# Two hybrid layers on one core: Exp per head with its own sum, value matmuls over four heads at once, and an expert stage that adds x at its end

## The chip, the cores and the metric

The program runs as one launch on one core of a Trainium2 chip. The metric is the device time of that launch in microseconds (us), as the median of several executions. A core has a matrix engine (TensorE, PE in the profile, with its weight loads as PEld), a vector engine (DVE), a scalar engine (ACT), GpSimd (POOL) and a queue engine that here only starts DMAs (SP). Each runs its own list of instructions in order; semaphores tie them together. Working memory is SBUF (128 partitions); matmuls write to PSUM, eight banks of 128 x 512 float32.

## The reference, cut to what matters

Activations are 256 tokens of width 1024 (`N`, `D`), kept with the features on the partitions as eight tiles of 128 x 256 (`KD` = 8). A first network of two layers (feed-forward, Fourier mixer, retention) runs first, then a second network of two layers. Only the second is changed. One of its layers does, in order:

```
u = rmsnorm(x, ln1);   p = u @ w_in                       # ProjectIn
attention, 2 groups of 4 heads, 4 branches                 # Attention
    s = q k^T / 8 + bias                                   # compressed, selected, window: gated
    w = exp(s - max(s)) / sum(exp(s - max(s)))             # sliding window with a sink per head:
    o = sum over the branches of gate * w @ v              #   max and sum include the sink
rwkv branch;  merge of the branches;  x = x + merged @ w_out
z = rmsnorm(x, ln2)                                        # expert_norm
route: top 16 of 128 x 128 keys per head                   # PeerRoute, PeerGates
x = x + sum over 128 blocks of (gates * gelu(z @ U_b)) @ V_b   # PeerExperts
```

After the second layer comes a last rmsnorm, and its result is the output.

## The kernel before, in words

The program is a list of stages (`second_network`, L2676). Each stage has one method per engine, and each engine runs the methods of all stages one after the other. `stage_done` counts finished stages; most methods begin by waiting for it. All large products are split into float32r parts: `product` (L240) issues three matmuls (L243 to L245) where one would do: rounded weights by rounded input, rounded weights by the input's rest, rest of the weights by rounded input. Weights come as blocks of 1 MB through a ring of four, loaded by SP; ACT rounds a block (L231, in `lead` ahead of a stage's start) and POOL subtracts to get the rest (L259).

`Attention` (L1302) works in 16 units: for each tile of 128 queries (t = 0, 1) and each group g of four heads there are the branches CMP (15 compressed keys), SEL, WIN and SWA. A unit's width is 15 keys for CMP, otherwise 128 keys at t = 0 and 256 at t = 1. PE issues, for u = 0 to 15, `scores(u + 3)` (L1411), `turn(u)`, which transposes the weights (L1423), and `values(u - 1)` (L1443), which does something only after WIN (with CMP, SEL and WIN summed in PSUM) and after SWA. DVE issues `shift(u + 1)` ahead of `weigh(u)`: shift is scale and bias (L1544), maximum (L1546), for CMP a clamp (L1548), for SWA the sink (L1551, L1552), and the subtraction (L1553); weigh is the sum (L1562) and four-number operations (L1564 to L1572). ACT issues `exp(u + 2)` (L1471), `keep(u)` (L1478), which copies the transposed weights out of PSUM, and `keep_sum(u - 1)` (L1487). POOL multiplies the weights by their scale (L1588). Scores are plain float32, so each matmul of attention appears in the trace as two records.

`Norm` (L448) squares x on ACT (L488), sums on PE (L519, L522), takes the root on ACT (L493) and the reciprocal on DVE (L543), scales (L559), rounds on ACT (L507) and takes the rest on DVE (L552). Where the stage before is a `Project`, its ACT part is early: it starts with each pair of tiles of x. Otherwise it waits for the whole stage.

The experts sum into PSUM banks 4 to 7, two tiles of x per bank. Before, `expert_norm` puts x there first with four matmuls by the identity (L531), because it then overwrites the other half of `chip.x`; all 128 blocks add to it without closing the sum; at the end four matmuls by a block of zeros close the banks (L2586), and one DVE copy moves all eight tiles to `chip.x` (L2663). The stage `LoadTables` (L1183) then starts two DMAs from ACT, for masks and the bias table of attention, ahead of the next norm.

## Time and profile before

| | |
|---|---|
| median of 3 runs | 5032.56 us (5031.7 to 5032.76) |
| the profiled execution | 5030.94 us |
| its span, first to last instruction | 5028.8 us |
| PE busy | 4589.3 us, 91% of the span |
| DVE / ACT / POOL busy | 33% / 34% / 56% |
| attention of the second network, layer 0 | about 2174 to 2286 us |
| attention, layer 1 | about 3704 to 3817 us |
| last expert matmul of layer 0 / layer 1 | ends at about 3480.0 / 5007.9 us |

The profile is of one execution, and its times are from the span's start. In the rows, a line number is a line of this kernel; "idle" and the arrow say how long an engine stood still before an instruction and what released it. PEclk is the granted clock of TensorE as a share: 0.50 is 1.2 GHz and 1.00 is 2.4 GHz.

### The profile page before, as it was taken

The page shows a single profiled execution, that of the slowest core. Times are in us where ns is not written, and L with a number is a line of the kernel's source. Part 1 is how long each engine was busy: PE and PEld are TensorE (multiplying, and loading weights), DVE is VectorE, ACT ScalarE, POOL GpSimd, SP SyncE. Part 2 cuts the span into 40 slices and gives each one's busy share as a digit, 9 for nine tenths or more (in the row PEclk, how much of TensorE's full clock was granted, in tenths as well). Part 3 has the DMA queues.
Part 4 walks back from the last instruction along what each step waited for, and adds up shares of the span by engine and source line. Part 5 has one row for each costly group of instructions (what it writes and reads, how often), then busy time and mean ns, then how long its engine had stood idle before and what let it go on. Part 6 is the DMA issues. An engine that isn't in the chain of part 4 may idle for free.

```text
span 5028.8 us, 73099 instructions
## 1 busy us (share of the span) xinstructions
PE 4589.3 (91%) x30266; PEld 4143.0 (82%) x30266; DVE 1634.7 (33%) x3051; ACT 1727.8 (34%) x2481; POOL 2802.4 (56%) x1354
## 2 busy tenths in 40 slices
PE   7998999999999898998857999999998866999998
PEld 5777677787788798977857999998977865999998
DVE  2211221121114321464577111112454668111112
ACT  3223222222232343421224444444431233444443
POOL 3342343344344386720467888886730367888886
PEclk9999999999999899967888999999976888999999
DMA  6623364222232244410120555554420130454543
GB/s 259 233 92 84 117 247 163 84 101 92 84 109 101 84 168 163 168 67 1 59 101 22 180 182 184 184 182 174 167 100 1 48 112 1 176 184 183 180 181 141
DMA packets 94372, 648.52 MB, mean 129 GB/s; under 512 B 9824, under 2 KB 16224, under 8 KB 16608
## 3 DMA queue, kind: packets, MB, share of 16 engines
q1 hardware_dynamic: 87120, 633.21, 34.6%
q10 hardware_dynamic: 7056, 12.49, 1.1%
q8 instruction: 148, 2.42, 0.2%
q14 instruction: 48, 0.39, 0.0%
HBM read 641.46 MB, written 4.19 MB: 128 GB/s over the span
## 4 chain that ended last, share of the span: by engine, by line
PE 83%; DVE 12%; ACT 2%; issue 1%; POOL 1%; DMA 1%; SPq 0%; ACTq 0%; DVEq 0%; POOLq 0%
PE ps L243 23%; PE ps L244 23%; PE ps L245 22%; PE ps L2505 3%; PE ps L1443 2%; PE ps L398 1%; PE ps L1411 1%; DVE arena L2075 1%; DVE x L729 1%; PE ps L1762 1%; PE ps L1809 1%; PE ps L971 1%; DMA arena<-in_mod_weights 1%; PE ps L1423 1%; PE ps L1815 1%
## 5 line engine op out<-in xcount | busy, mean ns | idle before, releaser
L259 POOL TENSOR_TENSOR ring_rest<-ring,rounded 128x1024 fp32r<-128x1024 f32 x1032 | 2508.2, 2453 | 1635.6 <-ACT rounded L231 1366.7
L243 PE MATMUL ps<-part,rounded 128*128 128x256 f32 (+1 forms) x5760 | 1839.6, 319 | 108.0 <-DVE part L552 46.6
L244 PE MATMUL ps<-part,rounded 128*128 128x256 f32 (+1 forms) x5760 | 1827.5, 317 | 0.0
L245 PE MATMUL ps<-part,ring_rest 128*128 128x256 f32 (+1 forms) x5760 | 1826.0, 317 | 0.0
L243 PEld LDWEIGHTS ps<-part,rounded 128*128 128x128 f32 x5760 | 1111.3, 193 | 213.3 <-DVE part L552 43.5
L245 PEld LDWEIGHTS ps<-part,ring_rest 128*128 128x128 f32 x5760 | 1110.8, 193 | 68.8
L244 PEld LDWEIGHTS ps<-part,rounded 128*128 128x128 f32 x5760 | 1111.9, 193 | 66.9
L231 ACT ACTIVATE rounded<-ring 128x1024 fp32r<-128x1024 f32 x528 | 527.5, 1050 | 700.4 <-PE ps L245 693.5
L243 PE MATMUL ps<-x_parts,rounded 128*128 128x256 f32 x2304 | 655.9, 285 | 9.6 <-DVE x_parts L552 8.1
L2623 ACT ACTIVATE rounded<-ring 128x1024 fp32r<-128x1024 f32 x504 | 531.5, 1054 | 373.6 <-DMA ring<-in_weights 366.5
L244 PE MATMUL ps<-x_parts,rounded 128*128 128x256 f32 x2304 | 654.2, 284 | 0.0
L245 PE MATMUL ps<-x_parts,ring_rest 128*128 128x256 f32 x2304 | 654.1, 284 | 0.0
L243 PEld LDWEIGHTS ps<-x_parts,rounded 128*128 128x128 f32 x2304 | 444.4, 193 | 12.2 <-DVE x_parts L552 10.4
L244 PEld LDWEIGHTS ps<-x_parts,rounded 128*128 128x128 f32 x2304 | 444.6, 193 | 0.0
L245 PEld LDWEIGHTS ps<-x_parts,ring_rest 128*128 128x128 f32 x2304 | 444.6, 193 | 0.0
L2653 DVE TENSOR_TENSOR ps<-ps,arena 128x256 f32<-128x256 f32 x256 | 160.1, 625 | 680.0 <-ACT ps L2602 680.0
L2656 DVE TENSOR_TENSOR part<-ps,part 128x256 fp32r<-128x256 f32 x256 | 108.8, 425 | 520.4 <-ACT part L2608 520.4
L648 ACT ACTIVATE arena<-ps 128x512 f32<-128x512 f32 (+1 forms) x88 | 47.9, 544 | 617.8 <-PE ps L245 617.8
L662 DVE TENSOR_TENSOR part<-ps,arena 128x512 f32<-128x512 f32 (+1 forms) x88 | 55.0, 625 | 562.9 <-ACT arena L648 562.9
L2602 ACT ACTIVATE ps<-ps 128x256 f32<-128x256 f32 x256 | 94.2, 368 | 413.2 <-PE ps L245 413.2
L729 DVE SCALAR_TENSOR_TENSOR x<-ps,mods_of_layer,x 128x256 f32<-128x256 f32 x80 | 31.9, 476 | 512.0 <-PE ps L245 512.0
L2161 POOL TENSOR_TENSOR part<-arena,part 128x1024 fp32r<-128x1024 f32 x6 | 14.4, 2402 | 294.1 <-ACT part L2141 294.1
(325 smaller groups left out, 4408.3 us busy)
## 6 DMA issues: line engine op xcount, KB each, us to landing
ring<-in_weights SPq DMA_DIRECT2D x528, 1024.0 KB, 4.8
arena<-in_mod_weights SPq DMA_DIRECT2D x72, 1024.0 KB, 7.8
arena<-bias_scratch ACTq DMA_DIRECT2D x2, 2048.0 KB, 8.7
bias_scratch<-arena ACTq DMA_DIRECT2D x1, 3072.0 KB, 32.8
x<-in_x SPq DMA_DIRECT2D x1, 2048.0 KB, 10.0
arena<-in_keys ACTq DMA_DIRECT2D x2, 1024.0 KB, 5.0
arena<-in_cst SPq DMA_DIRECT2D x1, 1216.0 KB, 28.2
arena<-in_expo ACTq DMA_DIRECT2D x1, 1024.0 KB, 4.8
```

The source lines that it names most:

```text
L231: self.nc.scalar.activation(c.rounded[:, s % ROUNDED, half], c.ring[:, slot, half], ACT.Copy)\
L243: mm(out, w[0], a[0], start=start, stop=False)
L244: mm(out, w[0], a[1], start=False, stop=False)
L245: return mm(out, w[1], a[0], start=False, stop=stop)
L259: eng.tensor_tensor(c.ring_rest[:, slot, half], c.ring[:, slot, half], c.rounded[:, (self.s0 + r) % ROUNDED, half].bitcast(F32), ALU.subtr ...
L729: last = self.nc.vector.scalar_tensor_tensor(c.x[:, m, cols], c.ps[:, m, cols], gate, c.x[:, m, cols], ALU.mult, ALU.add)
L1443: last = nc.tensor.matmul(ps[:, 6 + n % 2, i * P:(i + 1) * P], v, weights, start=k == 0, stop=k == len(parts) - 1)
L2505: last = self.nc.tensor.matmul(self.chip.ps[:, n % self.BANKS, i * P:(i + 1) * P], self.hot[:, n % self.BUFS, 0, i], self.hot[:, n % self. ...
L2602: copy(self.hidden(r), c.ps[:, r % 2, 0:N], ACT.Gelu).then_inc(self.gelu_ready.sem, 1)
L2623: self.nc.scalar.activation(c.rounded[:, (self.s0 + r) % ROUNDED, half], c.ring[:, f % RING, half], ACT.Copy)\
L2653: v.tensor_tensor(gelu, gelu, self.gates[:, :, bass.ds(b, 1)].rearrange("p t a -> p (t a)"), ALU.mult)\
L2656: v.tensor_tensor(self.parts[1][:, r % 2, :], gelu, self.parts[0].bitcast(F32)[:, r % 2, :], ALU.subtract)\
```

## The change

Attention: the subtraction of the maximum is gone from DVE; the maximum is taken with its sign turned and given to ACT as the bias of Exp, and since a bias is one number per partition, Exp is issued once for each of the four heads, each with an accumulator output that is the sum over the keys. DVE's sum is gone as well. The value matmuls take all four heads' weights as one moving operand of 512 columns instead of four of 128.

Experts: x is no longer put into PSUM. `expert_norm` copies it in SBUF (seven tiles into the arena, the eighth over the modulation table, which is now one tensor for both layers and no longer needed by then). Four float32r matmuls with zeros open the banks before the first block adds to them. The last block closes its sums itself and signals after each bank, and DVE adds x tile by tile. A norm behind the experts is early, as behind a `Project`. `LoadTables` is no stage any more; its two DMAs are issued by ACT at the end of the norm.

```diff
@@ Norm
-        early = isinstance(self.before, Project)
+        early = isinstance(self.before, (Project, PeerExperts))
...
-        if self.keep:
-            act.wait_ge(self.x_kept.sem, self.x_kept.at(1))
...
+        if self.tables:
+            self.tables.issue(act)
...
-        if self.keep:
-            for b in range(4):
-                last = mm(c.ps[:, 4 + b, :].rearrange("p (m n) -> p m n", m=2), c.ident, c.x[:, 2 * b:2 * b + 2, 0:N],
-                          start=True, stop=False)
-            last.then_inc(self.x_kept.sem, 1)
...
         dve.wait_ge(self.chip.stage_done, self.index)
+        for tiles, kept in self.kept or ():
+            nc.vector.tensor_copy(kept, c.x[:, tiles, 0:self.t])
         dve.wait_ge(self.summed.sem, self.summed.at(1))
@@ Attention
-            for i in range(4):
...
-                for k, (v, weights) in enumerate(parts):
-                    last = nc.tensor.matmul(ps[:, 6 + n % 2, i * P:(i + 1) * P], v, weights, start=k == 0, stop=k == len(parts) - 1)
+            for k, (v, weights) in enumerate(parts):
+                last = nc.tensor.matmul(ps[:, 6 + n % 2, :], v, weights.rearrange("p i t -> p (i t)"),
+                                        start=k == 0, stop=k == len(parts) - 1)
...
-            e = self.sc[:, u % self.BUFS, :, 0:self.width(t, b)]
-            nc.scalar.activation(e, e, ACT.Exp).then_inc(self.exped.sem, 1)
+            for i in range(4):
+                e = self.sc[:, u % self.BUFS, i, 0:self.width(t, b)]
+                last = nc.scalar.activation(e, e, ACT.Exp, bias=st[:, 0, i:i + 1], accum_out=st[:, 1, i:i + 1])
+            last.then_inc(self.exped.sem, 1)
...
-            link(v.tensor_reduce(st[:, 0, :], sc, AX.X, ALU.max))
+            last = v.tensor_reduce(st[:, 0, :], sc, AX.X, ALU.max, negate=True)
...
-            v.tensor_tensor(sc, sc, st[:, 0, :].unsqueeze(2).broadcast_to([P, 4, w]), ALU.subtract)\
-                .then_inc(self.shifted.sem, 1)
+            last.then_inc(self.shifted.sem, 1)
...
             dve.wait_ge(self.exped.sem, self.exped.at(u + 1))
-            link(v.tensor_reduce(st[:, 1, :], sc, AX.X, ALU.add))
@@ PeerExperts
+def kept_input(chip):
+
+    most = KD - 1
+    mods = chip.all_mods[:].rearrange("p l a d s -> p (l a d s)")[:, 0:N].rearrange("p (d n) -> p d n", d=1)
+    return [(slice(0, most), chip.at(G_KEPT, most, N)), (slice(most, KD), mods)]
...
+                if end and m % 2 and m < KD - 1:
+                    last.then_inc(self.closed.sem, 1)
...
+            if r == 1:
+                pe.wait_ge(self.zeroed.sem, self.zeroed.at(1))
+                for bank in range(4, 8):
+                    nc.tensor.matmul(c.ps[:, bank, :], self.zero[:, 0:P], self.zero, start=True, stop=False)
...
-        for bank in range(4, 8):
-            last = nc.tensor.matmul(c.ps[:, bank, :], self.zero, c.cst[:], start=False, stop=True)
-        last.then_inc(self.closed.sem, 1)
...
-        dve.wait_ge(self.closed.sem, self.closed.at(1))
-        v.tensor_copy(c.x[:, :, 0:N], c.ps[:, 4:8, :].rearrange("p b (m n) -> p (b m) n", n=N)).then_inc(c.stage_done, 1)
+        for m in range(KD):
+            if m == KD - 2:
+                dve.wait_ge(c.block_done, self.block_count(self.blocks - 1))
+            elif m % 2 == 0:
+                dve.wait_ge(self.closed.sem, self.closed.at(m // 2 + 1))
+            for tiles, x in self.kept:
+                if tiles.start <= m < tiles.stop:
+                    v.tensor_tensor(c.x[:, m, 0:N], x[:, m - tiles.start, :], self.out(m), ALU.add)\
+                        .then_inc(self.x_ready.sem, 1)
```

The places in the order of instructions on which the steps of the prediction rest follow, before and then now. Names of tiles: `ps` is PSUM, `arena` the SBUF work area, `part` a float32r tile in it, `cst` the constants. Line numbers of the changed kernel differ slightly.

PE in attention at t = 1 from the scores of unit 13 (L1411) to the values behind the last unit (L1443):

```order
L1411 MATMUL ps<-arena 128x256 x4
L1423 MATMUL ps<-cst,arena 128x128 x8
L1443 MATMUL ps<-arena 128x128 x20
L1411 MATMUL ps<-arena 128x256 x4
L1423 MATMUL ps<-cst,arena 15x128 x4
L1443 MATMUL ps<-arena 128x128 x8
L1423 MATMUL ps<-cst,arena 128x128 x24
L1443 MATMUL ps<-arena 128x128 x28
```

```order
L1407 MATMUL ps<-arena 128x256 x4
L1419 MATMUL ps<-cst,arena 128x128 x8
L1438 MATMUL ps<-arena 128x512 x5
L1407 MATMUL ps<-arena 128x256 x4
L1419 MATMUL ps<-cst,arena 15x128 x4
L1438 MATMUL ps<-arena 128x512 x2
L1419 MATMUL ps<-cst,arena 128x128 x24
L1438 MATMUL ps<-arena 128x512 x7
```

The order is the same; each group of value matmuls has a quarter of its number, with four times the columns.

DVE at the same stretch: shift of the sliding-window unit 11, weigh of unit 10, then shift of unit 12.

```order
L1544 SCALAR_TENSOR_TENSOR arena<-ps,arena 128x1024
L1546 TENSOR_REDUCE arena<-arena 128x4
L1551 TENSOR_TENSOR arena<-arena,vec 128x4
L1552 TENSOR_TENSOR arena<-vec,arena 128x4
L1553 TENSOR_TENSOR arena<-arena 128x1024
L1562 TENSOR_REDUCE arena<-arena 128x4
L1566 TENSOR_SCALAR arena<-arena 128x4
L1567 RECIPROCAL arena<-arena 128x4
L1572 TENSOR_TENSOR arena<-arena 128x4
L1544 SCALAR_TENSOR_TENSOR arena<-ps,arena 128x4x15
```

```order
L1543 SCALAR_TENSOR_TENSOR arena<-ps,arena 128x1024
L1545 TENSOR_REDUCE arena<-arena 128x4
L1552 SCALAR_TENSOR_TENSOR arena<-vec,arena 128x4
L1553 TENSOR_TENSOR arena<-vec,arena 128x4
L1564 TENSOR_SCALAR arena<-arena 128x4
L1565 RECIPROCAL arena<-arena 128x4
L1570 TENSOR_TENSOR arena<-arena 128x4
L1543 SCALAR_TENSOR_TENSOR arena<-ps,arena 128x4x15
```

Two of the four wide operations between one unit's scores and the other unit's scale are gone (L1553 and L1562 of before). On ACT the one Exp of each unit became four, in the same place.

DVE at the end of the experts and in the norm behind them:

```order
L2663 COPY x<-ps 128x8x256
L541 COPY arena<-ps 128x256
L543 RECIPROCAL ps<-arena 128x256
L559 SCALAR_TENSOR_TENSOR arena<-x,vec,ps 128x256 x8
L2789 UNCONDITIONAL_BRANCH
```

```order
L2679 TENSOR_TENSOR x<-arena,ps 128x256 x7
L2679 TENSOR_TENSOR x<-mods,ps 128x256
L540 COPY arena<-ps 128x256
L542 RECIPROCAL ps<-arena 128x256
L558 SCALAR_TENSOR_TENSOR arena<-x,vec,ps 128x256 x8
```

The one wide copy became eight adds of one tile each, of which six wait only for the first three banks.

## Rows read from the trace of the kernel before

**Rows 1.** Two stretches of attention: length, busy per engine, PEclk, DMA share, GB/s

```profile
2174.00:2286.00 112.00, 102.94 (x392) 82.98 (x392) 60.40 (x124) 27.24 (x44) 18.73 (x16) 0.55 0.01 3
3740.00:3760.00 20.00, 20.00 (x56) 13.99 (x56) 9.79 (x16) 3.90 (x5) 3.22 (x3) 0.50 0.00 0
```

**Rows 2.** Order of time, PE, attention: start, length, instruction, idle before

```profile
2186.77 1.11 PE L1423 MATMUL ps<-cst,arena 128*128 128x128 f32 x4 [1.16 <-POOL arena L1588]
2219.04 7.56 PE L1443 MATMUL ps<-arena 15*128 15x128 f32 x24
2238.25 1.09 PE L1423 MATMUL ps<-cst,arena 128*128 128x128 f32 x8 [1.33 <-POOL arena L1588]
2244.52 10.98 PE L1443 MATMUL ps<-arena 15*128 15x128 f32 x40
2259.96 3.62 PE L1443 MATMUL ps<-arena 128*128 128x128 f32 x16
2267.14 1.97 PE L1423 MATMUL ps<-cst,arena 128*128 128x128 f32 x8 [2.63 <-POOL arena L1588]
```

**Rows 3.** Chain that ended last behind layer 0's experts: start, length, where

```profile
3480.00 3.45 PE ps L2586 x8
...
3483.48 2.30 DVE x L2663
...
3486.75 0.13 ACT arena L488
...
3488.94 1.89 ACT rounded L231 x2
...
3492.14 0.48 ACT arena L493
```

**Rows 4.** The same behind the experts of layer 1, to the end

```profile
5007.90 3.45 PE ps L2586 x8
...
5018.87 0.48 ACT arena L493
```

**Rows 5.** The chain through the norm ahead of the routing, layer 0

```profile
2530.06 3.45 PE ps L531 x8
...
2533.98 2.39 DVE x_parts L552
```

**Rows 6.** Order of time, DVE, around unit 11

```profile
2230.35 1.22 DVE L1544 SCALAR_TENSOR_TENSOR arena<-ps,arena 128x1024 f32<-128x1024 f32 x1 [6.76 <-PE ps L1411]
2233.25 1.23 DVE L1553 TENSOR_TENSOR arena<-arena 128x1024 f32<-128x1024 f32 x1
2234.40 1.21 DVE L1562 TENSOR_REDUCE arena<-arena 128x4 f32<-128x1024 f32 x1
```

**Rows 7.** Order of time, ACT: four pieces with bias; then around exp 15

```profile
2147.80 1.57 ACT L1843 ACTIVATE arena<-ps,vec 128x256 f32<-128x256 f32 x4 [2.20 <-PE ps L1670]
2263.62 0.59 ACT L1487 ACTIVATE arena<-ps 64x512 f32<-64x512 f32 x1 [2.83 <-PE ps L1443]
2264.21 1.04 ACT L1471 ACTIVATE arena<-arena 128x1024 f32<-128x1024 f32 x1
2265.15 1.00 ACT L1478 ACTIVATE arena<-ps 128x1024 f32<-128x1024 f32 x1
```

**Rows 8.** PEclk around the values of unit 11, in stretches of 2 us

```profile
2260.00:2262.00 2.00, 2.00 (x11) 2.00 (x11) 1.90 (x4) 0.59 (x1) 0.00 (x0) 0.50 0.00 0
2264.00:2266.00 2.00, 0.52 (x5) 0.28 (x3) 1.73 (x5) 2.00 (x4) 0.80 (x1) 1.00 0.00 0
```

**Rows 9.** Order of time where a norm is early already, behind a Project

```profile
1945.19 0.28 PE L245 MATMUL ps<-part,ring_rest 128*128 128x256 f32 x1
1946.32 0.63 ACT L488 ACTIVATE arena<-x 128x512 f32<-128x512 f32 x1 [0.15 <-DVE x L729]
1948.96 0.47 ACT L493 ACTIVATE arena<-ps,vec 128x256 f32<-128x256 f32 x1 [0.71 <-PE ps L522]
```

**Rows 10.** Order of time, first expert block to sum into PSUM

```profile
2748.26 0.36 PE L243 MATMUL ps<-part,rounded 128*128 128x256 f32 x1 [0.71 <-DVE part L2656]
```

More of the change, by code:

```diff
@@ L131, in __init__ @@
         self.headones, self.iota = self.cst[:, 2, :], self.cst[:, 3, :]
-        self.mods = [self.place(f"mods_of_layer{i}", [P, N_MOD, KD, 2])[0] for i in range(DEPTH)]
+        self.all_mods, = self.place("mods", [P, DEPTH, N_MOD, KD, 2])
+        self.mods = [self.all_mods[:, i] for i in range(DEPTH)]
         self.ps = ctx.enter_context(nc.psum_tensor("ps", [P, 8, 512], F32))
@@ L454, with __init__ @@
     TILE = 32
-    def __init__(self, chip, out, sq, small, tokens, bank, mod=None, gain=None, parts=None, keep=False, mods=None, lead=None):
+    def __init__(self, chip, out, sq, small, tokens, bank, mod=None, gain=None, parts=None, kept=None, tables=None, mods=None,
+                 lead=None):
         super().__init__(chip)
-        self.t, self.mod, self.gain, self.keep = tokens, mod, gain, keep
+        self.kept, self.tables = kept, tables
+        self.t, self.mod, self.gain = tokens, mod, gain
         self.mods, self.first_mods = mods, lead
@@ L2563, in up, with down @@
             last.then_inc(self.up_done.sem, 1)
-        def down(it, r):
+        def down(it, r, end=False):
             b = it * RING + r
@@ L2645, in dve @@
         dve.wait_ge(self.chip.stage_done, self.index)
-        v.memset(self.zero, 0.0).then_inc(self.zeroed.sem, 1)
+        v.tensor_scalar(self.zero, c.cst[:].rearrange("p a n -> p (a n)"), 0.0, None, ALU.mult).then_inc(self.zeroed.sem, 1)
         def body(it, first=False):
@@ L2681, in second_network @@
         tables = LoadTables(chip, start)
-        stages += [tables, second_norm(chip, columns(vec, "ln1", layer, KD), split=True), ProjectIn(chip),
+        stages += [second_norm(chip, columns(vec, "ln1", layer, KD), split=True, tables=tables), ProjectIn(chip),
                    Attention(chip, layer, tables), Rwkv(chip, layer)]
```

56 lines of the change are left out of this document (29 added, 27 removed).

## The prediction, made before the changed kernel ran

> **What bounds the kernel now.** I read the page first: PE is busy for 91% of the span and holds 83% of the chain that ended last, so a change pays only where it shortens PE's own work or a stretch in which PE stands. Then I looked at attention in windows, because all that the change does to DVE and ACT lies there. It takes 112 us per layer, and PE is busy for 102.9 of them, at a mean granted clock of 0.55; a piece of 20 us has PE busy throughout at 0.50, which is 1.2 GHz [rows 1]. So attention is bound by a slowly clocked PE, with a few waits. PE's timeline names these: it waits for POOL, 1.16 us near the start, 1.33 us ahead of turn 10 and 2.63 us ahead of turn 14 [rows 2]. Last come the chains behind the experts, where PE has nothing to do: from the last expert product to the root of the next norm there are 12.1 us in layer 0 and 11.0 us in layer 1 [rows 3, 4].
>
> **Values, four heads at once.** Two rows give the price of a record. 24 records take 7.56 us and 40 take 10.98 [rows 2]; both contain eight records with a stationary tile of 15 rows, so 16 full ones cost 3.42, or 0.214 each, and the eight cost 0.517 each, 0.30 more, which I read as a weight load that isn't hidden when the number of rows changes. Afterwards the groups have 6 and 10 records of 512 columns, two of them with 15 rows. The trace has such a record at 2.4 GHz: eight in 3.45 us, 0.431 each [rows 5], hence 0.863 at 1.2 GHz. 6 x 0.863 + 2 x 0.30 = 5.8 and 10 x 0.863 + 0.6 = 9.2: 1.77 us less each. There are four such groups per layer (units 2, 6, 10, 14): 7.1 us per layer. The sliding-window groups only swap 16 x 0.214 for 4 x 0.863, nothing. Bounds at an unchanged clock: 0.6 less per group if the penalty is paid per column and not per load, 0.6 more if it vanishes; 4.7 to 9.5 per layer.
>
> **DVE, ACT and the waits.** Unit 11 shows why PE waits. Its shift can start only with its scores at 2230.35, and weigh of unit 10 stands behind it in DVE's queue, so L1553 (1.23) and L1562 (1.21) both lie between the scores and the scale of unit 10 [rows 6]. Both go, about 2.4 us. Against that ACT issues four Exps. Four 256-column activations with a bias take 1.57 together [rows 7], against 1.04 for the one Exp now. What an accumulator output adds isn't in this trace. It can't be under 0 (0.39 per piece), and the nearest row for one more small activation, L1843's own 0.39, gives 0.8 per piece as the other end. I take 0.15 more, 0.55 per piece, 2.2 per unit at 256 keys, because it moves four bytes per partition. Behind exp on ACT's queue stand keep and keep_sum; turn of the next unit waits for keep. So:
> - Start: DVE no longer paces the first units; the wait of 1.16 goes. ACT needs less than 3 us per unit there, PE as much. Gain 1.2.
> - Turn 10: weigh 10 is ready 2.4 earlier; ACT starts exp 11 when unit 7's keep_sum is out, ends it 2.2 later and then keeps unit 9, just before PE comes. Gain 1.3.
> - Turn 14: here ACT takes over. exp 15 starts behind keep_sum 11 (2263.62), now 2264.21, and keep 13 (2265.15) stands behind it [rows 7]. With 2.2 in place of 1.04 keep 13 ends at about 2267.3, and turn 14 began at 2267.14. So of 2.63 us of wait nothing comes back: 0.
> Per layer 2.5, with ends of -1.5 (0.8 per piece) and 4.
>
> **The clock inside attention.** PE busy isn't enough for 2.4 GHz: 20 us at full busy share were granted 0.50 [rows 1]. It does rise during the 16 records of unit 11's values, dense and with 128 rows: 0.50 at 2260, 1.00 at 2264 [rows 2, 8]. In the 40 records ahead of them, interrupted eight times, it doesn't. Merged, the full rows stand together: 8 x 0.863 = 6.9 us in one piece for unit 10, and 10.4 for units 14 and 15, against 3.6 at unit 11. I expect the clock to rise inside both. For unit 10 that saves 1 to 2 us in the values, up to 1.9 in the scores of unit 15 and some of the chain behind; for the last group 2 to 3. The shorter groups of units 2 and 6 (3.4 us dense) may go either way. I take 5.5 per layer from ends of 0 and 12. The Trainium skill ("TensorE: Matmul & The Clock Gate", section "What's actually happening") says that a hardware monitor sets the clock by how busy PE has been and that activity releases the throttle. Read as busy time this is not what the trace shows [rows 1], and by it merging would change nothing in the clock: that is the first rival below.
>
> **Behind the experts.** In layer 0 the last product ends at 3480.00; then come the closing matmuls (3.45), the copy (2.30), 0.97 in which ACT issues the tables' DMAs, the squares, two roundings, a table load and the root at 3492.14 [rows 3]: 12.14 us. Afterwards three banks are closed before the last product ends, and two adds remain, as behind a Project. There the last product ends at 1945.31, the last square runs from 1946.32 to 1946.95 and the root starts at 1948.96 [rows 9]. So the squares end 1.64 after the products, and what follows the squares on ACT is unchanged, 3492.14 - 3488.94 = 3.20 [rows 3]: the root comes at 4.84, 7.3 earlier. At the end there is no rounding: 5018.87 - 5007.90 = 10.97 becomes 3.65, again 7.3 [rows 4, 9]. The norm that opens the second network loses only the DMA issues, 0.9. The DMAs themselves now start at the end of ACT's norm and still have some 200 us until attention; behind them in ACT's queue stand only roundings whose slots aren't free yet. 15.5 together.
>
> **Ahead of the routing, and the zeros.** L531 (3.45) held ACT's first rounding until 2533.5, so that the first rest started at 2533.98 and then stood for 2.39 beside POOL's subtraction [rows 5]. Without it the rest can slip in ahead of that operation of POOL, and PE gets one tile of the queries earlier, though at 1.2 GHz and with the next tile as late as before: 0.7 per layer. The two copies on DVE fill a gap there of about 1.4 us with some 1.3; if they don't fit, the gain is gone (0) or a whole POOL operation, 2.4, is lost once per layer. The four zero matmuls stand ahead of the first sum into PSUM, where PE waits 0.71 us for DVE now [rows 10]; each is one pass over 512 columns where the records of 0.43 [rows 5] are two, so 0.22 to 0.43 each, 0.9 to 1.7 less 0.7 together: I take 0.2 per layer. Together 1.0.
>
> **Sum.** 2 x (7.1 + 2.5 + 5.5) = 30.2 in attention, 15.5 behind the experts, 1.0 for the rest: 46.7. From the profiled execution's 5030.94 that is 4984.2; the median of the runs shown lies 1.6 above that execution, so I predict 4986.
>
> **Rivals.**
> - *The clock stays.* The scores with their 64 rows and the turns break the dense pieces, or the monitor looks at something that merging leaves as it is. For: no rise in 20 us of full busy share. Against: the rise at unit 11. 11 us less gain: 4997.
> - *ACT takes the place of DVE.* Each Exp piece with its accumulator costs about 0.95, more than twice a plain piece. Then exp 15 takes 3.8, keep 13 ends 1.8 us later than turn 14 began, turn 10 is 0.3 later, and the first units run at ACT's pace, 2 later: the waits cost 4 per layer where I gain 2.5. 13 us less: 4999, or 5004 if the clock suffers too.
> - *The clock rises in all four groups* and stays for the scores between them. For: merged, the full rows of units 2 and 6 are 3.5 us in one piece, about what unit 11 has now. Against: their scores of 64 rows come right behind. 8 us per layer more: 4970.
> - *Slower than before.* One mechanism only has the size: ACT bounds attention as a whole. It issues 64 Exp pieces per layer, beside what it does now, 27.2 us at most [rows 1]. To eat the other terms (15.5 and 1.0) and 10 us more, attention would have to last 13 us longer per layer, 125 us, so (125 - 27) / 64 = 1.5 us per piece, four times the 0.39 of a plain one. A table load ahead of each piece would do it, but the order of instructions has one load per layer there. It would give 5043, and decides from 1.5 us per piece.
>
> **How the numbers follow.** Forecast 0.62, clock stays 0.17, ACT 0.09, clock everywhere 0.08, slower 0.02, something unseen 0.02. The range of 8 in 10 takes in the first two whole and most of the next: 4968 to 5003. A measurement of this kernel tells 0.2% (10 us) from no change; nearly all cases are beyond it: faster 0.96, same 0.02, slower 0.02.
>
> **What would show it.** Right: value records of 0.86 us at 0.50, six and ten to a group; PEclk near 1.00 in the later half of unit 10's values; no wait ahead of turn 10, a wait for ACT's keep ahead of turn 14; Exp pieces of 0.4 to 0.8; the root 4.8 and 3.7 us behind the last expert product; attention at 95 to 99 us. Wrong: attention above 105, pieces near 1 us, or a first query product that isn't earlier against the norm's root.

## The result, and the profile after

The changed kernel takes 4960.16 us (median of 4, 4957.67 to 4961.43), against 5032.66 for the kernel before on the same chip: ratio 0.9855, interval 0.9838 to 0.9872. That is 72.5 us less where I forecast 46.7, and below my range. The profiled execution took 4957.67, its span 4955.9, 72.9 less than before. By milestones of the two traces, forecast in the last column:

| stretch | before | after | difference | forecast |
|---|---|---|---|---|
| start to last square behind the first network's last Project | 1946.32 | 1944.32 | -2.0 | 0 |
| to the first scores of layer 0 | 229.3 | 227.4 | -1.9 | -0.9 |
| attention, layer 0 | 110.5 | 84.3 | -26.2 | -15.1 |
| to the last product ahead of the routing's norm | 240.7 | 241.8 | +1.1 | 0 |
| to the first query product | 9.6 | 10.1 | +0.5 | -0.7 |
| to the last expert product | 943.6 | 942.9 | -0.7 | +0.2 |
| to the first product of layer 1 | 17.3 | 9.9 | -7.3 | -7.3 |
| to the first scores of layer 1 | 208.0 | 208.1 | +0.1 | 0 |
| attention, layer 1 | 112.0 | 81.3 | -30.8 | -15.1 |
| to the last expert product | 1190.6 | 1192.2 | +1.6 | -0.5 |
| to the end | 20.9 | 13.6 | -7.3 | -7.3 |

Attention is the whole miss: 57.0 against 30.2. Its windows, first the layer 0 stretch and then layer 1 (columns as in [rows 1]), and layer 1 of before, which [rows 1] lacks:

```profile
2171.00:2256.00 85.00, 78.35 (x260) 48.96 (x260) 34.77 (x91) 43.33 (x156) 18.75 (x16) 0.69 0.00 1
3669.00:3750.00 81.00, 75.18 (x260) 46.89 (x260) 34.56 (x88) 42.98 (x156) 18.75 (x16) 0.71 0.00 1
```

```profile
3705.00:3817.00 112.00, 103.86 (x392) 83.81 (x392) 59.50 (x121) 27.23 (x44) 18.74 (x16) 0.55 0.00 1
```

DVE's work fell from 60 to 35 us, ACT's rose from 27 to 43, and the granted clock rose from 0.55 to 0.69 and 0.71. Length times clock gives attention in microseconds at full clock: 112.0 x 0.55 = 61.6 before, 85.0 x 0.69 = 58.7 and 81.0 x 0.71 = 57.5 after. At the old mean clock of 0.55 these would be 106.7 and 104.5 us. So by this reckoning 5 and 7 us per layer are less work and waiting, and the rest of 26 and 31, some 21 and 23, is clock. (It is rough: a wait does not scale with the clock.) Over the whole span the clock records of the two traces give 758 us at 1.2 GHz before and 653 after; half of the difference, 52.6 of the 72.9 us, is clock. PE in layer 0, in order of time, columns as in [rows 2], which these answer:

```profile
2171.73 7.19 PE L1407 MATMUL ps<-arena 64*128 64x15 f32 x32 [6.14 <-DVE arena L1526]
2181.63 1.11 PE L1419 MATMUL ps<-cst,arena 128*128 128x128 f32 x4
...
2188.77 5.78 PE L1438 MATMUL ps<-arena 15*128 15x512 f32 x6
...
2211.52 5.78 PE L1438 MATMUL ps<-arena 15*128 15x512 f32 x6
2217.23 1.99 PE L1407 MATMUL ps<-arena 64*128 64x256 f32 x8
...
2225.53 1.06 PE L1419 MATMUL ps<-cst,arena 128*128 128x128 f32 x8 [0.97 <-ACT arena L1477]
...
2229.47 4.75 PE L1438 MATMUL ps<-arena 15*128 15x512 f32 x10
...
2242.30 1.06 PE L1419 MATMUL ps<-cst,arena 128*128 128x128 f32 x8 [3.03 <-ACT arena L1477]
2244.57 1.94 PE L1419 MATMUL ps<-cst,arena 128*128 128x128 f32 x8 [1.21 <-ACT arena L1477]
...
2256.01 0.66 PE L1738 MATMUL ps<-cst,arena 128*128 128x128 f32 x4 [0.73 <-ACTq L1500]
```

The reader is to see that the values of units 2 and 6 take the forecast 5.8 at 1.2 GHz, that scores of 256 keys behind unit 6 take 1.99 and no longer 3.78, so the clock is up 45 us behind the first scores and stays up through the values of units 10 and 11 and the scores of unit 15; and that the wait ahead of turn 14 is there, now for ACT. Behind that wait the clock falls: the last turn takes 1.94 for 1.06.

Behind the experts of layer 0 (chain that ended last), and at the end of the program; they answer to [rows 3, 4]:

```profile
3448.84 2.92 DVE x L2679 x8
...
3452.32 1.99 ACT rounded L232 x2
...
3455.61 0.48 ACT arena L495
```

```profile
4942.22 0.28 PE L246 MATMUL ps<-part,ring_rest 128*128 128x256 f32 x1
4942.43 2.20 PE L521 MATMUL ps<-arena,cst 128*32 128x256 f32 x16
4942.87 0.41 DVE L2679 TENSOR_TENSOR x<-mods,ps 128x256 f32<-128x256 f32 x1
...
4945.96 0.47 ACT L495 ACTIVATE arena<-ps,vec 128x256 f32<-128x256 f32 x1 [0.71 <-PE ps L524]
```

The last products of the two layers are done at 3450.81 and 4942.35 (a record's successor begins 0.12 to 0.13 behind it): the root comes 4.8 and 3.6 later, forecast 4.8 and 3.7.

Ahead of the routing my gain of 0.7 became a loss of 0.5. The chain that ended last there, and POOL beside it:

```profile
2495.52 2.88 DVE x L728 x8
...
2498.55 2.02 DVE arena L538
2500.57 2.00 DVE mods L538
2502.57 0.34 DVE arena L540
...
2503.70 0.48 ACT arena L495
...
2508.22 2.13 DVE x_parts L551
```

```profile
2500.08 4.70 POOL L260 TENSOR_TENSOR ring_rest<-ring,rounded 128x1024 fp32r<-128x1024 f32 x2 [7.67 <-ACT rounded L232]
```

The copy of seven tiles begins before POOL does and takes 2.02 us; the eighth, a seventh of that, takes 2.00, until the first of POOL's two operations (4.70 / 2, begun at 2500.08) is over.

### The profile page after: what moved, and what is told of

The parts are those of the page before. It is cut to its first block, busy times and chain, and to the rows that moved or that the text cites. A ratio compares the mean times of both kernels' runs of the same rounds, so it can differ in the third digit from the quotient of the medians.

```text
span 4955.9 us, 72697 instructions
## 1 busy us (share of the span) xinstructions
PE 4523.0 (91%) x29978; PEld 4068.8 (82%) x29978; DVE 1591.1 (32%) x3005; ACT 1760.5 (36%) x2705; POOL 2803.8 (57%) x1354
## 4 chain that ended last, share of the span: by engine, by line
PE 83%; DVE 12%; ACT 2%; issue 1%; POOL 1%; DMA 1%; SPq 0%; DVEq 0%; ACTq 0%; POOLq 0%
PE ps L244 23%; PE ps L245 23%; PE ps L246 23%; PE ps L2511 3%; PE ps L399 1%; PE ps L1407 1%; PE ps L1438 1%; DVE arena L2073 1%; DVE x L728 1%; PE ps L1760 1%; PE ps L1807 1%; PE ps L970 1%; DMA arena<-in_mod_weights 1%; PE ps L1419 1%; ACT rounded L232 1%
## 5 line engine op out<-in xcount | busy, mean ns | idle before, releaser
L728 DVE SCALAR_TENSOR_TENSOR x<-ps,mods,x 128x256 f32<-128x256 f32 x80 | 31.9, 475 | 511.6 <-PE ps L246 511.6
L664 DVE TENSOR_TENSOR part<-part,part 128x512 fp32r<-128x512 f32 (+1 forms) x88 | 129.6, 1473 | 142.5 <-ACT part L651 142.5
```

The costliest lines, as they stand in the source:

```text
L664: v.tensor_tensor(self.parts[1][:, j, :], self.h[:, j, :], self.parts[0].bitcast(F32)[:, j, :], ALU.subtract)\
L728: last = self.nc.vector.scalar_tensor_tensor(c.x[:, m, cols], c.ps[:, m, cols], gate, c.x[:, m, cols], ALU.mult, ALU.add)
```

## The experiments

Each edit is against the kernel before or the changed one, as its first words say. "Rise" is where PEclk goes to 1.00, counted from the first scores. The attention lengths are of one profiled execution each, the medians of four or more.

| kernel | median us | attention layer 0 / 1 | rise |
|---|---|---|---|
| before | 5032.7 | 110.5 / 112.0 | 57 / 57 |
| only values merged | 5005.7 | 91.5 / 91.2 | 30 / 30 |
| only heads inner, not merged | 4991.2 | 91.7 / 91.3 | 30 / 30 |
| only Exp per head | 4985.1 | 85.8 / 85.7 | 30 / 30 |
| only experts | 5010.1 | 101.9 / 110.5 | 32 / 57 |
| before, 1 us shift | 5039.6 | 112.1 / 115.0 | 57 / 90 |
| before, 2 us shift | 5029.1 | 112.9 / 101.9 | 90 / 32 |
| changed | 4960.2 | 84.3 / 81.3 | 45 / 23 |
| changed, 1 us shift | 4964.4 | 81.4 / 74.5 | 23 / 22 |
| changed, values per head | 4987.6 | 96.9 / 85.8 | 56 / 30 |

**Theories.** 1: the merged, dense value records bring the clock. 2: the absence of waits brings and holds it. 3: where it rises is decided by where attention falls in time, and each length is a draw: it changes with small shifts of the stage, though the code of attention stays the same.

**Only the values merged.** The kernel before with the diff's merged loop over `parts` and nothing else.

> The kernel before with nothing but the value matmuls merged over four heads. Exp, DVE's work and the experts are as before. Theory 1 (dense records): the merged records themselves raise PE's clock one or two groups of values earlier than I forecast, and that is where the 26 us beyond my forecast came from. Then most of attention's gain of 57 us is here: the 7.1 per layer of fewer records and 12 to 16 per layer of clock, 4985 to 4995 in all, with a stretch of PEclk 1.00 from the values of unit 2 or 6 on. Theory 2 (waits): the clock rises because PE no longer stands still for POOL. Then this run keeps the clock of before, 0.50 to the end of unit 6's values and beyond, and gains the records alone, 14 us: 5018.

5005.7, ratio 0.9947 (0.993 to 0.9964). Attention gains 19 and 21 us, with the early rise of theory 1; the time gains only 26.7, because later stages give some back: from the end of attention to the next first scores it is 1424.4 us against 1419.1, and from the end of layer 1's attention to the last product 1199.0 against 1190.6. Attention of layer 0 in pieces, then two waits of PE in it:

```profile
2176.00:2205.00 29.00, 27.31 (x92) 19.19 (x92) 20.16 (x53) 6.97 (x14) 4.73 (x6) 0.50 0.00 1
2205.00:2223.00 18.00, 16.44 (x77) 11.04 (x77) 16.63 (x32) 7.02 (x12) 4.26 (x4) 0.97 0.00 1
2223.00:2241.00 18.00, 16.13 (x38) 9.26 (x38) 14.49 (x26) 5.54 (x7) 5.96 (x4) 0.53 0.00 0
```

```profile
2221.05 1.09 PE L1423 MATMUL ps<-cst,arena 128*128 128x128 f32 x8 [1.56 <-POOL arena L1588]
2222.07 2.90 PE L1411 MATMUL ps<-arena 64*128 64x256 f32 x8
2226.84 1.97 PE L1423 MATMUL ps<-cst,arena 128*128 128x128 f32 x8 [1.87 <-POOL arena L1588]
```

The clock fell between these two waits for POOL: the scores between them take 2.90, neither 1.99 nor 3.78.

**Only the order of heads.**

```diff
-                for k, (v, weights) in enumerate(parts): matmul(... i * P ..., v, weights)
+            for k, (v, weights) in enumerate(parts):
+                for i in range(4):
+                    last = nc.tensor.matmul(ps[:, 6 + n % 2, i * P:(i + 1) * P], v, weights[:, i, :],
+                                            start=k == 0 and i == 0, stop=k == len(parts) - 1 and i == 3)
```

> The kernel before, where the value matmuls keep their 128 columns and one head each, but the loop over heads is the inner one: eight records with 15 rows first, then all with 128 rows in one piece. Number and width of records are as before. Theory 1a (one dense piece of 128-row records raises the clock, however wide they are): PEclk as in the run with merged values only, and by way of the clock 10 us or more per layer less: about 5005 to 5012. Theory 1b (it is the 512 columns per weight load): the clock stays as before, and at most the 0.30 us penalty of the interrupted loads comes back, 1.8 per group, four groups per layer: 5018 to 5033.

4991.2, 0.9917 (0.9901 to 0.9934), one execution at 5000 and three at 4991. Twenty-four records of 128 columns in this order take 5.78 us, as six of 512 do:

```profile
2196.69 5.78 PE L1443 MATMUL ps<-arena 15*128 15x128 f32 x24
```

Attention comes out as with merging, 91.7 and 91.3. So what helps is that the 15-row tile no longer interrupts, and width adds nothing that can be seen: theory 1a, and 1b falls. The medians of the two differ by 14 us. Their profiled executions differ by 4.9, none of it in attention: the stretch behind layer 1's attention took 1192.1 us here and 1199.0 with merging, with the same instructions. What made three executions 9 us faster than the profiled one isn't known.

**Only Exp.** The kernel before with the diff's Exp and its edits on DVE.

> The kernel before with nothing but Exp per head with its accumulator, and without DVE's subtraction and sum. Values and experts are as before. Theory 1 (dense records): the waits go as in the changed kernel, the clock does not change, 2 to 3 us per layer: 5026 to 5029. Theory 2 (waits): PE without waits gets its clock earlier, 10 us or more per layer: 5005 to 5012.

4985.1, 0.9906 (0.989 to 0.9923). This is the run that my forecast missed most: 25 and 26 us of attention by Exp's part alone, with the old value records.

```profile
2176.00:2206.00 30.00, 29.77 (x119) 25.09 (x119) 13.15 (x43) 14.43 (x64) 5.48 (x7) 0.50 0.00 1
2206.00:2242.00 36.00, 33.09 (x203) 26.61 (x202) 20.78 (x45) 24.57 (x89) 11.16 (x9) 1.00 0.00 1
2242.00:2262.00 20.00, 17.14 (x72) 14.71 (x72) 0.40 (x2) 4.08 (x5) 2.10 (x2) 0.57 0.00 1
```

PE is busy for 29.8 of the first 30 us (the waits of [rows 2] near the start are gone), the clock rises and is held for 36 us, past a wait of 0.94 ahead of turn 10, to the wait of 2.96 ahead of turn 14. By the clock records PE is at 1.2 GHz for 656 us of this span, where before it was 758: half of that difference, 51, is more than the whole gain.

**Only the experts.** The changed kernel with attention as before.

> The changed kernel with attention as before: the expert part, the early norm behind it and the tables' DMAs at the end of the norm are what is left. My terms gave 15.5 us behind the experts; the trace of the changed kernel has 0.9 for the DMAs, 7.4 and 7.4 for the norms, and about 1.2 lost by the second kept copy on DVE ahead of the routing, twice 0.5 to 0.6. Theory 1 and 2 alike: 5018, within 2. If the two parts help each other (a clock that rises at another time because the experts end at another), it comes out at 5010 or 5025 instead.

5010.1, 0.9956 (0.9939 to 0.9973), 8 us under the expectation, and layer 0's attention accounts for it: 101.9 us for instructions that took 110.5 in the kernel before. The three separate gains (26.7, 47.3, 22.3) sum to 96.3, where together they give 72.5. That led to theory 3.

**Shifts.** One more square on ACT in each norm ahead of attention, result unused (4 tiles; 8 in the second):

```diff
+            if d == KD - 2 and self.parts and self.mod is None and not self.keep:
+                nc.scalar.activation(c.at(B_P, 4, N), c.x[:, 0:4, 0:N], ACT.Square)
```

> The kernel before, with one more activation on ACT (a square of four tiles of x, about 1.04 us, result unused) in the norm ahead of each second-network ProjectIn, so that both attentions start 1 us later against all that went before. Nothing in attention changes. So far the same attention code took 110.6 and 112.1 us (before) but 102.0 in layer 0 and 110.5 in layer 1 of the run with only the expert part changed; it differed in where the clock rose, 30 or 56 us behind the first scores. Theory 3 (phase): where the clock rises depends on when attention starts, so a shift of 1 us alone can move a layer's attention by 9 us. It says: at least one of the two layers at about 102, total 5018 to 5026; if both flip, 5016. Theory 2 (waits inside attention alone decide): both stay at 110 to 112, total 5034.5.

> As the last, with a square of eight tiles, about 2.1 us. Theory 3 (phase): the pattern of the clock is different again from that with 1 us, and a layer's attention comes out at either about 102 or about 111; any of 5018, 5027, 5036. Theory 2: 110 to 112 in both layers, 5036.7.

5039.6, 1.0012 (1.0003 to 1.0022; the profiled execution is the slowest of ten), and 5029.1, 0.9992 (0.9982 to 1.0002): 1 us of work per layer costs 6, 2 us per layer cost nothing that can be measured. The layers differ by more than the edit. In the second kernel, the first 89 us of layer 0 and then the start of layer 1:

```profile
2179.00:2268.00 89.00, 87.31 (x304) 69.01 (x305) 53.63 (x110) 21.64 (x36) 14.95 (x14) 0.50 0.00 1
3712.00:3742.00 30.00, 28.31 (x113) 23.73 (x114) 19.52 (x52) 6.96 (x14) 4.73 (x6) 0.50 0.00 1
3742.00:3764.00 22.00, 19.49 (x109) 15.26 (x108) 20.39 (x39) 9.17 (x15) 5.65 (x5) 0.96 0.00 0
```

The same instructions, 1533 us apart: in one layer 0.50 for 89 us, in the other 0.96 from 30 us on. Length 112.9 against 101.9. My number for the first kernel (a layer at 102) missed, since it drew 112.1 and 115.0; that theory 2's 110 to 112 twice fails in both kernels stands.

> The changed kernel with the same additional square of four tiles. Theory 3 (phase): attention's 84.3 and 81.2 us are draws too. The runs with only Exp or only values changed had the rise at 30 us in both layers, here it came at 45 and 22. With a rise at 30 that stays (no wait for POOL) the length should be under 80: the total could drop to 4952 though ACT has 2 us more to do, or rise by up to 10 to 4972. Theory 2 (waits alone): the attentions stay within 1 us of 84.3 and 81.2, and the total is 4962.

4964.4, 0.9865 (0.9848 to 0.9881); attention 81.4 and 74.5 in the profiled execution, the fastest of four. Theory 2 alone falls here too.

**Changed, with dense work in the wait ahead of the scores.**

```diff
+        for _ in range(3):
+            nc.tensor.matmul(ps[:, 6, :], self.chip.ident, self.chip.cst[:], start=True, stop=True)
         pe.wait_ge(self.cmp_kept.sem, self.cmp_kept.at(1))
```

> The changed kernel with three more float32 matmuls of 512 columns by a full 128-row tile (two records each, some 5.2 us at 1.2 GHz), results unused, in the 6.1 us in which PE waits for DVE's copies ahead of the first scores. They lie in a wait, so they cost nothing by themselves. If dense 128-row work raises the clock and work without waits holds it, PEclk is 1.00 soon after the first scores and mostly stays; PE's work in attention at 2.4 GHz is then near 60 us, less than DVE and ACT need beside it, and attention takes 68 to 76 us per layer: 4938 to 4950. If the 64-row scores bring the clock down again, attention stays at 81 to 84: 4960.

4948.7, 0.9832 (0.9815 to 0.9848): 11 us less than the changed kernel for work that is thrown away. The clock is up at the first scores but falls 1 to 3 us behind them, and rises again at 20 to 22 us (the three matmuls themselves take 2.84 us, at full clock, for the 5.2 that I had estimated); attention 80.1 and 71.9.

**Changed, values per head again.**

> The changed kernel with the value matmuls per head again, 128 columns each; all else stays changed. At a given clock the records cost 7.1 us more per layer (24 in 7.56 for 6 in 5.78, 40 in 10.98 for 10 in about 9.2). The clock so far: with Exp changed alone it rose 31 us behind the first scores in both layers and stayed 36 us, attention 85.8 twice; with both changes 84.3, 81.2, 81.4, 74.5, mean 80.4. Theory A (the waits that Exp's part takes away hold the clock, merging adds its records and little clock): attention at 84 to 88, total 4967 to 4972. Theory B (merging's dense records are needed as well): attention above 92, total over 4980.

4987.6, 0.9909 (0.9892 to 0.9925). Layer 1 is theory A's 85.8; layer 0 has its rise at 56 us and took 96.9. The expected total, 4972 at most, missed by 16 us: that layer is 9 above the expected 88, and some 14 us more than in the changed kernel went where nothing had been edited (4.2 in the first network, 4.3 and 5.8 behind the two attentions).

**Changed, no accumulator.** `accum_out` left out.

> The changed kernel whose Exp has no accumulator output; the sum over the keys is not computed at all, DVE goes on with a constant. This is the price of the accumulator by itself: in the changed kernel a piece of 256 keys takes 0.49 us with a read of the accumulator behind it, and my nearest row for a plain one was 0.39. Expected: pieces 0.39 apart, so exp 15 is 0.4 us shorter, and the waits ahead of turns 10 and 14 (0.97 and 3.03) shrink by 0.3 to 0.5 each; by themselves 1.5 us for both layers, 4958. If a shorter wait ahead of turn 10 keeps the clock up (theory A), up to 10 per layer more: 4945. If the accumulator costs nothing, pieces stay at 0.49.

4964.8, 0.9863 (0.9847 to 0.988). Exp 15 of the changed kernel, one piece of four, and all four without accumulator:

```profile
2239.19 0.49 ACT L1469 ACTIVATE arena<-arena 128x256 f32<-128x256 f32 x1
2239.59 0.18 ACT L1469 ACTIVATION_READ_ACCUMULATOR arena<-arena 128x1 f32 x1
2239.69 0.49 ACT L1469 ACTIVATE arena<-arena 128x256 f32<-128x256 f32 x1
```

```profile
2243.22 1.69 ACT L1469 ACTIVATE arena<-arena 128x256 f32<-128x256 f32 x4
```

Pieces are 0.49 apart with the read and 0.40 without. The waits ahead of turns 10 and 14 go from 0.97 and 3.03 to 0.60 and 2.66, as expected. Attention is 7.1 us shorter in the profiled execution (84.3 and 74.2), and the time still does not fall: against the changed kernel's execution the first network took 4.4 us more, the stretches behind the two attentions 3.3 and 7.0, all with unedited instructions.

**Changed, keep 9 ahead of exp 11.** In ACT's loop `keep(u)` moves ahead of `exp(u + 2)` for u = 9.

> The changed kernel with one swap on ACT: the copy of unit 9's turned weights stands ahead of Exp of unit 11 in place of behind it. PE's wait of 0.97 us ahead of turn 10 should go, and nothing else. Theory A (short waits bring the clock down): in three of four attentions of the changed kernel the clock fell right behind that wait, so without it the clock stays to the wait of 3.03 ahead of turn 14, and attention takes 72 to 78: 4945 to 4952. Theory 3 (phase alone decides when it falls): 0.97 less per layer, 4958, with attentions scattered over 74 to 84 as before.

4958.3, 0.9849 (0.9832 to 0.9865); 86.3 and 74.5. A wait of 0.53 for POOL takes the place of the 0.97. In the five profiled kernels that have the changed kernel's attention, or that and the three dense matmuls, the clock fell behind the 0.97 in four layers of ten; in the three with this swap in none of six. That fits theory A; the comparison at the end of this section says where it holds.

**Changed, compressed keys and values copied by ACT.** The copies L1525 and L1526 go from `dve` to `act`, behind the copy of the hidden units.

> The changed kernel with the copies of the compressed keys and values out of PSUM moved from DVE to ACT. On DVE they stand behind two operations of 3.35 and 2.91 us (1.2 us each where POOL does not run beside them), and PE waits 6.1 us for them; ACT has nothing to do there. The first scores should start about 5 us earlier against the last compression product, but DVE's first shift still stands behind the two operations, so only the 2.0 us between the first scores and the first shift, and some of the scores' 7.2, are saved: 2 to 4 us per layer, 4953 to 4957, and by the phase of the clock 10 us either way.

4951.9, 0.9837 (0.9821 to 0.9854). The wait is 0.73 us where it was 6.14, and part of it comes back as 1.21 for DVE. Counted from the first scores, which come 5.4 and 4.9 us earlier in their stage, attention took 75.9 and 82.5.

```profile
2171.19 3.78 PE L1407 MATMUL ps<-arena 64*128 64x15 f32 x16 [0.73 <-ACT arena L1464]
2176.18 1.22 PE L1407 MATMUL ps<-arena 64*128 64x128 f32 x4 [1.21 <-DVE arena L1544]
```

**Changed, the eighth tile kept by ACT.**

```diff
+        if self.kept:
+            tiles, kept = self.kept[1]
+            nc.scalar.activation(kept, c.x[:, tiles, 0:self.t], ACT.Copy)
         act.wait_ge(self.mean.sem, self.mean.at(1))
```

> The changed kernel, where the eighth tile of x is kept by ACT ahead of the root and no longer by DVE. In the changed kernel that DVE copy of 256 columns took 2.09 us, from 2500.49 to the end of an operation of POOL that had begun at 2500.08, and DVE's copy of the squares' sum stood behind it. Theory P (DVE's copy is held for as long as POOL's operation runs): without it the sum's copy comes about 1.9 us earlier and the first query product 1.5 to 1.9, in both layers: 4957. Theory Q (the copy is slow whatever POOL does, or PE's first product waits for something else, such as the rest on DVE beside POOL): less than 0.5 per layer, 4960. The clock of the attentions may add 7 to 10 us either way, so this is read from the distance of the last product of the merge to the first query product (9.96 us in the changed kernel).

4960.0, 0.9854 (0.9838 to 0.987). The sum's copy comes 2.0 us earlier, as theory P has it, but the first query product only 0.5 (9.6 behind the last product, 10.1 before the edit), as theory Q's numbers had it:

```profile
2503.00 0.41 DVE L544 COPY arena<-ps 128x256 f32<-128x256 f32 x1
...
2507.69 2.16 DVE L555 SCALAR_TENSOR_TENSOR x_parts<-x,x_parts 128x256 fp32r<-128x256 f32 x1
```

The first rest now starts inside one of POOL's operations and lasts 2.16, where it was 0.65 in the changed kernel. The hold has moved to the next DVE operation.

**Changed, late norm behind the experts.** `early` for `Project` alone.

> The changed kernel, where the norm behind the experts waits for the whole stage again instead of starting with each pair of tiles. The banks still close one by one. My term of 7.3 us was the distance of the last expert product to the root, 12.1 before and 4.8 now; it had the closing matmuls (3.45), the wide copy and the DMAs in it, and the squares beside the products. By the rows the squares then start behind the last add: the last of four ends 2.2 later than now less the last square's own 0.65, so the root comes at 6.3 to 6.6 in place of 4.8. 1.6 per layer: 4963. If the early norm is what brings most of it (say 4 or more per layer) it is 4968 or more.

4959.4, 0.9853 (0.9836 to 0.9869). The roots come 6.4 and 5.2 behind the last product, 1.6 later each, as expected; layer 1's attention took 74.2, 7.1 less than in the changed kernel, and so the time is the changed kernel's. So of 7.3 the closing banks and the queue give 5.7, the early norm 1.6.

**Two versions that beat both kernels.** ACT's two copies and keep 9 together, and that with the three dense matmuls:

> The changed kernel with three edits of this study together: compressed keys and values copied by ACT (4951.9 alone), the eighth tile of x kept by ACT, and the copy of unit 9's turned weights ahead of Exp of unit 11. By their own terms 8 + 3 + 1 us under the changed kernel's 4960: 4948, and the phase of the clock puts it anywhere from 4938 to 4956. A distribution of attention's length over 74 to 84 per layer is expected by theory 3.

> The last one with the three dense unused matmuls ahead of the first scores. There the wait that covered them is now shorter (the copies come about 5 us earlier), so they are on PE's path for 3 to 4 us per layer; in exchange the clock should be at 1.00 at the first scores, as for 3 us in the run where they stood in the wait. If the clock then holds (theory A), 4940; if it falls in the 64-row scores as it did there, the matmuls cost what they last: 4952 to 4956.

4943.8, 0.9821 (0.9805 to 0.9838), attention 75.6 and 75.7; 4937.8, 0.9808 (0.9791 to 0.9824), 73.4 and 74.8, executions from 4928 to 4941. The dense matmuls' six records take 2.84, at full clock. They put the first scores 3.3 us behind the start of the last compression records instead of 1.35, so they cost 2.0 here, and the first sixteen records of the scores give 1.7 of it back (2.05 for 3.78). Where the rest of the 6 us between the medians comes from isn't settled.

```profile
2167.50 2.84 PE L1400 MATMUL ps<-cst 128*128 128x512 f32 x6
2170.27 2.05 PE L1413 MATMUL ps<-arena 64*128 64x15 f32 x16
```

**The same code, sorted by the place of the clock.** In every trace whose first scores stand behind DVE's copies, with nothing put into the wait, the clock is up in the stage ahead of attention and falls 4.2 to 5.7 us ahead of the first scores, while PE waits. In the kernel before with the 2 us shift, from 6 to 4 us ahead of the first scores of layer 0 and of layer 1:

```profile
2172.85:2174.85 2.00, 0.05 (x1) 0.00 (x0) 2.00 (x1) 0.12 (x1) 2.00 (x2) 0.67 1.00 418
3705.86:3707.86 2.00, 0.00 (x0) 0.00 (x0) 2.00 (x1) 0.00 (x0) 2.00 (x2) 0.56 1.06 446
```

A mean of 0.67 over 2 us is 0.7 us at full clock, so the fall is 5.3 us ahead; 0.56 gives 5.7 or 5.8. Sorted by that distance, the attentions of the profiled executions fall into place (lengths in us; a column takes every layer with that code of attention, whatever was edited outside it):

| clock falls ahead of the first scores | before | merged, or heads inner | Exp per head only | changed |
|---|---|---|---|---|
| 4.2 to 4.4 | 110.5, 110.5 | 91.5, 91.7 | 85.8, 85.8 | 81.3, 81.4, 81.3 |
| 4.6 to 4.9 | 112.0, 112.1 | 91.2, 91.3 | 85.7 | 74.5 |
| 5.2 to 5.4 | 115.0, 112.9 | | | 74.2 |
| 5.7 | 101.9, 101.9 | | 96.9 | 84.3, 84.3, 84.3 |

So a length is no chance of the execution: where the distance is the same, it repeats within 0.2 us in every cell but one (115.0 and 112.9), and half a microsecond of distance moves it by up to 13. Read along a row, the parts can be told apart. At 4.2 to 4.4, values alone give 19, Exp alone 25 and both 29. At 5.7, Exp alone gives 5.0 and both 17.6. What one edit is worth depends on the place, and the parts don't add.

The waits can be compared in the same way. In the 4.2 to 4.4 row of the changed kernel the clock fell behind the wait of 0.97 ahead of turn 10 in all three layers. Keeping unit 9 first (0.53 for POOL, later) and leaving out the accumulator (0.60) each have a layer in that row too: there the clock held until the wait ahead of turn 14, and attention took 74.5 and 74.2 for 81.3. The two kernels with ACT's copies of keys and values have such a pair, layer 1, where the clock falls 0.4 and 0.5 us behind the first scores and rises 24 us behind them in both. From 44.7 to 49.7 us behind them, with the wait of 0.97 and with unit 9 kept first (82.5 and 75.7 us in all):

```profile
3700.00:3705.00 5.00, 5.00 (x16) 3.46 (x15) 1.83 (x6) 3.63 (x14) 1.26 (x2) 0.51 0.01 2
3699.00:3704.00 5.00, 4.47 (x20) 2.73 (x20) 4.83 (x9) 4.24 (x18) 2.18 (x2) 1.00 0.01 2
```

In the other rows of the changed kernel the same wait of 0.97 did not bring the clock down. So theories 2 and 3 hold together: a short wait costs the clock in one place and nothing in another.

## Why the prediction was wrong, and where it was right

- **The step that failed is "The clock inside attention": 5.5 us per layer from ends of 0 and 12.** It measured about 21 and 23. I tied the clock to the merged records alone, and read [rows 8] as: only dense records with 128 rows bring a rise. Exp's part alone, without merging, took 25 and 26 us, nearly all of it clock, off the layers where the clock fell 4.2 to 4.7 us ahead of the first scores, and 5 where it fell 5.7 ahead. I had priced its waits (2.5) and not what PE's clock does where the waits are gone. My own trace had a rise that doesn't fit my reading, 57 us behind the first scores, at the end of the eight records of unit 7's values; scores of 256 keys then take 1.99:

```profile
2231.07 1.92 PE L1443 MATMUL ps<-arena 128*128 128x128 f32 x8
2234.93 1.99 PE L1411 MATMUL ps<-arena 64*128 64x256 f32 x8
```

- **The upper end was no bound.** Of the 112 us PE was at 1.2 GHz for most, so a clock that is up throughout would give far more than 12. A bound estimated from the rows would have been 112.0 x 0.55 = 61.6 us at full clock, 50 us less.
- **A single trace was taken for the kernel.** The attention code of before took 102 to 115 us in eight layers of four profiled kernels, the changed one 74 to 84 in eight layers of four (changed, shifted, ACT's copy, late norm). The means, 109.6 and 80.7, differ by 29 per layer, so that there is a gain is no luck of one trace. How much of it a kernel shows is partly luck: 17.6 in a layer where the clock falls 5.7 us ahead, 29 at 4.2 to 4.4. The Trainium skill ("TensorE: Matmul & The Clock Gate", section "What's actually happening") calls the monitor's window free-running, so that the transition depends on where the work falls in it. The traces agree that the place of the work decides. That the window is free-running they do not show: a kernel's executions mostly repeat (19 of the kernel before lie within 4.3 us, where one layer alone can differ by 13). The section puts the effect under 1% of a typical kernel; here one layer's attention alone moved by 11 to 13 us, 10% of that stage and 0.2% of the kernel.
- **Rival 3 (the clock rises in all four groups) was right in kind**, and its 4970 too dear by 10: it did not rise in all four groups, but earlier in each layer and for longer, at the end of unit 6's values in layer 0 and of unit 2's in layer 1, 45 and 23 us behind the first scores.
- **Values:** 5.78 for the forecast 5.8. That the extra time goes with changes of the number of rows holds (with heads inner, eight such changes become two and 7.56 becomes 5.78); that it is a weight load is not shown. The group of ten was never at 1.2 GHz throughout, so its 9.2 stays unseen. The lower end of this term was wrong: a price paid per column would have cost the eight records' 2.4 again, 1.8 less gain per group and not 0.6, and left nothing of the 7.1.
- **Waits, in layer 0:** 1.7 at the start for 1.2 (both early waits gone); a wait of 0.97 ahead of turn 10, forecast none; 3.03 for ACT's keep ahead of turn 14 for 2.63. Together 1.7 for 2.5. A piece is 0.49 for 0.55. ACT as the bound, and slower than before, are ruled out by it.
- **Behind the experts:** 7.3 and 7.3 for 7.3 and 7.3, and 0.94 for the DMA issues forecast at 0.9: the first norm of the second network has its squares begin at 1953.90, 9.58 behind the last square of the norm before it, where it was 10.52.
- **Ahead of the routing:** a loss of 0.5 where I had 0.7 of gain. I had named the case, a whole operation of POOL, and given it too little: the second copy met it in full. The Trainium skill ("SBUF — State Buffer", section "Who interferes with whom") says that DVE in its two-port mode and GpSimd exclude each other for a whole instruction, whoever is first. The 2.00 us for 256 columns agree.
- **2.0 us before the change's first instruction and 1.0 ahead of attention** were not forecast. The first network has the same instructions in all eighteen kernels and took 1943.3 to 1948.2 us to its last product; the changed kernel's execution has the shortest. It was at 1.2 GHz for 139.9 us of that before and 136.5 after, 136.5 to 146.8 in the eighteen traces, and its length less half of this time is 1874 to 1877 in all of them. So the 2.0 is clock and belongs to no edit. The 1.0 is gone again in the changed kernel with the shift (208.2 us from the first product of ProjectIn to the first scores, as before, for 207.3); its cause isn't shown further. The stretch behind layer 1's attention, 1190.6 to 1199.2 in the traces, scatters too, so a difference of a few microseconds between two kernels' totals says little about an edit.

## What to carry to other kernels

Where PE's granted clock is half for most of a stage, price the clock first: length times clock gives the work at full speed, and the distance to it is what any edit that removes small waits can release. Do not take one trace's clock pattern as a property of the code; shift the stage by a microsecond or two, note how far ahead of the stage the clock fell, and compare two versions only where that distance is the same. And a copy on DVE that "fits a gap" needs the gap to be free of POOL's operations, since the next DVE operation may inherit the hold.

## What was unexpected of the hardware

- Identical attention code was granted 0.50 for 89 us in one layer and 0.96 from 30 us on in the other of the same execution. The clock had fallen 5.3 us ahead of the first scores in one and 5.7 in the other.
- Three thrown-away dense matmuls ahead of attention made the program 11 us faster (4960.2 to 4948.7, intervals of the ratio 0.9838 to 0.9872 and 0.9815 to 0.9848), though the clock they brought fell again within 3 us of the first scores.
- Exp's accumulator output appears as an instruction of its own of 0.18 to 0.19 us, and adds 0.09 to the spacing of pieces.
- Twenty-four value records took 7.56 or 5.78 us, both at 1.2 GHz, by their order alone.
